# Four of twelve merge gate units made among the recurrent heads, and attention groups with 96 instead of 144 gate products

## What is computed

```python
h = rmsnorm(x, g_pre_mix)
z = h @ w_in                                   # 1024 -> 8248 columns
q_nsa, kv_nsa, g_nsa, qkv_ml, if_ml, o_ml, q_mem, g_merge = split(z)
y_nsa = gated sum of compressed, selected and window attention   # 16 heads in 4 groups
h_ml  = mlstm_chunkwise(q_m, k_m, v_m, i_pre, logf)              # 4 recurrent heads, qk after conv and silu
y_ml  = sigmoid(o_ml) * rmsnorm_per_head(h_ml)
y_mem = memory_xattn(q_mem, mem, g_mem, w_mem_kv)                # 4 heads
gm = sigmoid(g_merge.reshape(B, S, 3, 1024))
y  = gm[0] * (y_nsa @ w_proj_nsa) + gm[1] * (y_ml @ w_proj_ml) + gm[2] * (y_mem @ w_proj_mem)
x  = x + rmsnorm(y @ w_out, g_post_mix)
h  = rmsnorm(x, g_pre_ffn); x = x + (silu(gate) * up) @ w_ffn_down
```

## Time and profile before

| | |
|---|---|
| median of 3 runs | 3139.21 us (3135.36 to 3140.19) |
| the profiled execution | 3136.1 us, its span 3134.3 us |
| mean granted clock of TensorE in it | 0.962 |
| PE busy | 93% of the span |
| front | 0 to 371 us |
| attention groups | 371 to 787 us, 102 to 106 us each |
| projections and output | 787 to 942 us |
| feed-forward and second part | from there to the end |

### The profile page before, as it was taken

One profiled execution on the slowest core, in us unless ns is written; L12 is line 12 of the kernel. 1 busy time (PEld: TensorE's weight loads), 2 busy tenths in 40 slices (PEclk: granted clock), 3 DMA queues, 4 the chain that ended last, 5 costly groups with the idle time before them and its releaser, 6 DMA issues.

```text
span 3134.3 us, 34634 instructions
## 1 busy us (share of the span) xinstructions
PE 2910.9 (93%) x13386; PEld 2382.4 (76%) x13386; DVE 1513.3 (48%) x2168; ACT 887.5 (28%) x1206; POOL 341.1 (11%) x70
## 2 busy tenths in 40 slices
PE   6998799999898999899997699999999889899997
PEld 6777688888776888778885588887888765578886
DVE  2334354445457443464534845444543379555532
ACT  4333343334233222222221322122222232332211
POOL 4222111111310000000000000000000056100000
PEclk9998899899999999999998899999999999999999
DMA  6221112221441232323222122332232221122232
GB/s 193 85 67 61 54 43 83 67 71 44 144 154 54 94 106 87 101 68 106 94 93 82 51 97 94 101 101 81 94 104 91 88 68 41 55 80 94 94 98 71
DMA packets 255085, 270.43 MB, mean 86 GB/s; under 512 B 5695, under 2 KB 243407, under 8 KB 254858
## 3 DMA queue, kind: packets, MB, share of 16 engines
q1 hardware_dynamic: 250688, 261.77, 26.1%
q10 hardware_dynamic: 4298, 7.36, 0.6%
HBM read 258.62 MB, written 10.49 MB: 86 GB/s over the span
## 4 chain that ended last, share of the span: by engine, by line
PE 69%; issue 16%; DVE 6%; POOL 5%; ACT 2%; DMA 1%; SPq 0%; POOLq 0%; DVEq 0%; ACTq 0%
PE bank L1114 20%; PE bank L1115 20%; PE bank L1116 20%; POOL w_lo L1074 3%; POOL w_lo L1068 3%; PE bank L1566 1%; PE bank L1129 1%; PE bank L1131 1%; PE bank L1130 1%; DVE rstd L1989 1%; ACT w_hi L662 1%; PE bank L1142 1%; PE bank L1144 0%; PE bank L1143 0%; DVE w_lo L1954 0%
## 5 line engine op out<-in xcount | busy, mean ns | idle before, releaser
L1114 PE MATMUL bank<-h_hi,w_hi 128*128 128x512 f32 x2064 | 817.5, 396 | 53.5 <-POOL w_lo L1074 25.1
L1115 PE MATMUL bank<-h_lo,w_hi 128*128 128x512 f32 x2064 | 811.3, 393 | 0.0
L1116 PE MATMUL bank<-h_hi,w_lo 128*128 128x512 f32 x2064 | 810.6, 393 | 0.0
L1954 DVE TENSOR_TENSOR w_lo<-w_raw,w_hi 128x2048 fp32r<-128x2048 f32 (+2 forms) x176 | 390.3, 2220 | 391.7 <-ACT w_hi L662 325.7
L1114 PEld LDWEIGHTS bank<-h_hi,w_hi 128*128 128x128 f32 x2064 | 392.6, 190 | 144.5 <-POOL w_lo L1074 29.3
L1116 PEld LDWEIGHTS bank<-h_hi,w_lo 128*128 128x128 f32 x2064 | 392.5, 190 | 83.1
L1115 PEld LDWEIGHTS bank<-h_lo,w_hi 128*128 128x128 f32 x2064 | 392.9, 190 | 82.5 <-issue 1.2
L1114 PE MATMUL bank<-hid_hi,w_hi 128*128 128x512 f32 x880 | 343.5, 390 | 0.0
L1116 PE MATMUL bank<-hid_hi,w_lo 128*128 128x512 f32 x880 | 342.4, 389 | 0.0
L1115 PE MATMUL bank<-hid_lo,w_hi 128*128 128x512 f32 x880 | 342.4, 389 | 0.0
L654 ACT ACTIVATE w_hi<-w_raw 128x2048 fp32r<-128x2048 f32 x124 | 237.0, 1911 | 356.7 <-PE bank L1116 349.3
(11 more groups left out here) (355 smaller groups left out, 3489.1 us busy)
## 6 DMA issues: line engine op xcount, KB each, us to landing
w_raw<-in_ffn_w_in_dram SPq DMA_DIRECT2D x88, 1024.0 KB, 5.1
w_raw<-in_w_in_dram SPq DMA_DIRECT2D x32, 1024.0 KB, 5.4
w_raw<-in_ffn_w_out_dram SPq DMA_DIRECT2D x32, 1024.0 KB, 5.1
w_raw<-in_w_ffn_in_dram SPq DMA_DIRECT2D x22, 1024.0 KB, 5.1
w_raw<-in_ffn_w_out_dram SPq DMA_DIRECT2D x16, 768.0 KB, 4.5
w_raw<-in_conv_w_pw_dram SPq DMA_DIRECT2D x12, 1024.0 KB, 5.5
w_raw<-in_w_ffn_down_dram SPq DMA_DIRECT2D x8, 1024.0 KB, 5.1
gate_scratch<-gate_stage ACTq DMA_DIRECT2D x24, 256.0 KB, 2.0
```

The source lines that it names most:

```text
L1114: nc.tensor.matmul(bank[b][:, 0:n], wh, xh, start=first, stop=False)
L1115: nc.tensor.matmul(bank[b][:, 0:n], wh, xl, start=False, stop=False)
L1116: ins = nc.tensor.matmul(bank[b][:, 0:n], wl, xh, start=False, stop=last)
L1954: v.tensor_tensor(w_lo[slot][:, 0:n], raw[s][:, 0:n], w_hi[slot][:, 0:n].bitcast(F32), ALU.subtract).then_inc(w_lo_ready, 1)
```

## The change

Four of the twelve merge gate units, those of the third branch (memory), one for each group, become units of the front. `UNITS` has 26 entries: three of the new ones stand between, or just behind, the units qk, v and o as numbers 20, 22 and 24, and the first is 17, ahead of the last qk unit. The unit for the attention gates moves ahead of vw. In `SCHEDULE` the units 20, 22 and 24 stand between the scores and the outputs of heads 0, 1 and 2, the second output-gate unit (25) between the outputs of head 2 and the scores of head 3, and `ml_scores(2)` directly follows `ml_norm(0)`. ACT evacuates such a unit with two copies and stores both tiles with one DMA.

In the groups 96 gate products remain in four tiles. The weights of the second branch are loaded and split as two half units of 128 columns each. The first of these is split right behind the query copies, ahead of step 0, instead of at step 2. 24 gate products stand ahead of the split queries, one behind each of the 16 pairs of compressed scores, one in each step (two at the first query block of each branch), 8 and 5 in the tail. The tiles are copied out ahead of step 0, at steps 6 and 25, and at the end. The next query unit is split at step 25 instead of 32. The compressed scores go to banks 7 and 1 instead of 0 and 1, and the wait for `y_split` stands ahead of them.

```diff
          ("in", C_KV, UC, "kc"), ("in", C_KV + 256, UC, "vc"), ("in", C_KV + 512, UC, "ks"), ("in", C_KV + 1024, UC, "kw"),
-         ("in", C_KV + 768, UC, "vs"), ("in", C_KV + 1280, UC, "vw"), ("gates", 0, P, "gate"), ("gates", P, P, "if"),
-         ("in", C_QK, UC, "qk"), ("in", C_QK + 256, UC, "qk"), ("in", C_QK + 512, UC, "qk"), ("in", C_QK + 768, UC, "qk"),
-         ("in", C_V, UC, "v"), ("in", C_V + UC, UC, "v"), ("in", C_O, UC, "o"), ("in", C_O + UC, UC, "o")]
+         ("in", C_KV + 768, UC, "vs"), ("gates", 0, P, "gate"), ("in", C_KV + 1280, UC, "vw"), ("gates", P, P, "if"),
+         ("in", C_QK, UC, "qk"), ("in", C_QK + 256, UC, "qk"), ("in", C_QK + 512, UC, "qk"), ("in", C_MERGE + 2 * D, UC, "merge"),
+         ("in", C_QK + 768, UC, "qk"), ("in", C_V, UC, "v"), ("in", C_MERGE + 2 * D + UC, UC, "merge"), ("in", C_V + UC, UC, "v"),
+         ("in", C_MERGE + 2 * D + 2 * UC, UC, "merge"), ("in", C_O, UC, "o"), ("in", C_MERGE + 2 * D + 3 * UC, UC, "merge"),
+         ("in", C_O + UC, UC, "o")]
 NFIX = len(UNITS)
-FEATURE_MAJOR = ("mem_k", "q_mem", "kc", "vc", "ks", "kw", "qk")
-ACT_ONLY = ("mem_v", "gate", "if", "o")
+FEATURE_MAJOR = ("mem_k", "q_mem", "kc", "vc", "ks", "kw", "qk", "merge")
+ACT_ONLY = ("mem_v", "gate", "if", "o", "merge")
+UNIT_OF, TURN_OF = {}, []
+for _u, (_, _, _, _kind) in enumerate(UNITS):
+    TURN_OF.append(len(UNIT_OF.setdefault(_kind, [])))
+    UNIT_OF[_kind].append(_u)
 DVE_EVACS = [0]
...
-             ("ml_const", 0), ("ml_rows", 0), ("unit", 15), ("unit", 16), ("unit", 17), ("ml_cols", 0), ("unit", 18),
-             ("ml_scores", 0), ("ml_out", 0), ("unit", 19), ("ml_scores", 1), ("ml_out", 1),
-             ("unit", 20), ("ml_gain", 0), ("ml_norm", 0), ("unit", 21), ("ml_scores", 2), ("ml_out", 2), ("ml_scores", 3),
-             ("ml_gain", 1), ("ml_out", 3), ("ml_norm", 1), ("ml_turn", 0)]
+             ("ml_const", 0), ("ml_rows", 0), ("unit", 15), ("unit", 16), ("unit", 17), ("unit", 18), ("ml_cols", 0),
+             ("unit", 19), ("ml_scores", 0), ("unit", 20), ("ml_out", 0), ("unit", 21), ("ml_scores", 1), ("unit", 22), ("ml_out", 1),
+             ("unit", 23), ("ml_gain", 0), ("ml_norm", 0), ("ml_scores", 2), ("unit", 24), ("ml_out", 2),
+             ("unit", 25), ("ml_scores", 3), ("ml_gain", 1), ("ml_out", 3), ("ml_norm", 1), ("ml_turn", 0)]
...
 GATE_BANK = (4, 0)
-GATE_TILES = 6
-GATE_PRE, GATE_STEP = 18, 3
-GATE_EVAC = {8: 0, 16: 1, 24: 2, 32: 3}
+GATE_TILES, ALL_TILES = 4, 6
+GATE_PRE, GATE_CMP, GATE_TAIL = 24, 1, (8, 5)
+GATE_STEP = [2 if qb == 0 else 1 for br, qb, hh in STEPS] + [1] * 3
+GATE_EVAC = {6: 1, 25: 2}
+HALF = KT * P
...
             with sp.Fori(0, GROUPS) as g:
-                def gate_load(b):
-                    load(g * 2 + (U_NSA // 2 + (b + 1) // 2), (b + 1) % 2, w_in_t[:, :, bass.ds(g * UC + (C_MERGE + b * D), UC)], KT, UC)
+                def half_gate_load(t):
+                    load(g * 2 + (U_NSA // 2 + 1), t, w_in_t[:, :, bass.ds(g * UC + (C_MERGE + D + t * P), P)], KT, P)
                 load(g * 2 + U_NSA // 2, 0, w_in_t[:, :, bass.ds(g * UC, UC)], KT, UC)
-                gate_load(0)
-                gate_load(1)
+                load(g * 2 + U_NSA // 2, 1, w_in_t[:, :, bass.ds(g * UC + C_MERGE, UC)], KT, UC)
+                half_gate_load(0)
+                sp.wait_ge(gt_front_stored, 16 * GROUPS)
                 sp.wait_ge(y_split, g * 2 + 2)
                 for b in range(2):
                     for i in range(2):
                         for half in range(2):
                             sp.dma_start(k_st[b][i][DH * half:DH * (half + 1), :].bitcast(F32),
                                          k_scratch[b, i, bass.ds(g * DH, DH), :]).then_inc(kd_landed, 16)
-                gate_load(2)
+                half_gate_load(1)
...
+                    act.wait_ge(evac_act, u + 1)
+                    g = TURN_OF[u]
+                    act.dma_start(g_scratch[g * ALL_TILES + 4:g * ALL_TILES + 6, :, :].rearrange("t p n -> p t n"), gt_front[:, :, :]
+                                  ).then_inc(gt_front_stored, 16)
                 if kind == "qk":
...
                     nc.scalar.activation(q_st[half, h, :], bank[0][half, :], ACT.Copy).then_inc(q_high, 1)
+                high_in_loop(g * 2 + (U_NSA // 2 + 1), 0, 0, HALF)
...
                 def gate_evac(m):
-                    if m % 2 == 0:
-                        act.wait_ge(gt_half, g * 3 + (m // 2 + 1))
+                    if m == 0:
+                        act.wait_ge(gt_half, g + 1)
                     else:
-                        act.wait_ge(w_used, g * 4 + (U_NSA + m // 2 + 2))
-                    act.wait_ge(gt_stored[m % 2], g * 48 + 16 * (m // 2 + 1))
+                        act.wait_ge(w_used, g * 4 + (U_NSA + m + 1))
+                    act.wait_ge(gt_stored[m % 2], g * 32 + 16 * (m // 2 + 1))
                     nc.scalar.activation(gt_stage[m % 2][:, :], bank[GATE_BANK[m % 2]][:, :], ACT.Copy).then_inc(gt_copied, 1)
                     act.wait_ge(gt_copied, g * GATE_TILES + (m + 3))
-                    act.dma_start(g_scratch[bass.ds(g * GATE_TILES + m, 1), :, :].rearrange("a p n -> p (a n)"),
+                    act.dma_start(g_scratch[bass.ds(g * ALL_TILES + m, 1), :, :].rearrange("a p n -> p (a n)"),
                                   gt_stage[m % 2][:, :]).then_inc(gt_stored[m % 2], 16)
+                gate_evac(0)
                 for i in range(NS + 2):
                     if i < NS:
...
-                    if i == 2:
-                        high_in_loop(g * 2 + (U_NSA // 2 + 1), 0, 0)
                     if i in GATE_EVAC:
                         gate_evac(GATE_EVAC[i])
                         if GATE_EVAC[i] == 1:
-                            high_in_loop(g * 2 + (U_NSA // 2 + 1), 1, 1)
-                        if GATE_EVAC[i] == 3:
+                            high_in_loop(g * 2 + (U_NSA // 2 + 1), 1, 1, HALF)
+                        if GATE_EVAC[i] == 2:
                             high_in_loop(g * 2 + (U_NSA // 2 + 2), 0, 0)
                 act.wait_ge(c_t, g + 1)
                 for qb in range(TT):
                     ins = nc.scalar.activation(pT_c[:, HPG * qb:HPG * (qb + 1), :],
...
+                gate_evac(3)
...
                 for n in range(4):
-                    low_in_loop(g * 4 + (U_NSA + 1 + n), (n + 1) % 2)
...
-                    b, t = m // 2, m % 2
-                    s, out_ = (b + 1) % 2, bank[GATE_BANK[t]][:, :]
+                    s, out_ = (1, 1, 0, 1)[m], bank[GATE_BANK[m % 2]][:, :]
+                    cols, c0 = (UC, m * P) if m < 2 else (P, 0)
                     if first == 0:
                         pe.wait_ge(gt_copied, g * GATE_TILES + (m + 1))
-                        if t == 0:
-                            pe.wait_ge(w_lo_ready, g * 4 + (U_NSA + 2 + b))
+                        if m != 1:
+                            pe.wait_ge(w_lo_ready, g * 4 + (U_NSA + max(m, 1) + 1))
                     for n in range(first, last):
                         k, part = n // 3, n % 3
-                        c = k * UC + t * P
+                        c = k * cols + c0
                         ins = nc.tensor.matmul(out_, (w_lo if part == 2 else w_hi)[s][:, c:c + P],
                                                (h_lo if part == 1 else h_hi)[:, k, :], start=n == 0, stop=n == 3 * KT - 1)
                     if last == 3 * KT:
-                        ins.then_inc(gt_half if t == 0 else w_used, 1)
+                        ins.then_inc(gt_half if m == 0 else w_used, 1)
...
                 pe.wait_ge(q_split, g + 1)
+                pe.wait_ge(y_split, g * 2 + 2)
...
                         c = NCP * (2 * qb + hh // 2)
-                        ins = stacked(bank[hh % 2][:, c:c + NCP], hh, qb, [kc_st[0][:, :], kc_st[1][:, :]])
-                ins.then_inc(c_s, 1)
+                        ins = stacked(bank[OUT_BANK[hh % 2]][:, c:c + NCP], hh, qb, [kc_st[0][:, :], kc_st[1][:, :]])
+                        if hh == HPG - 1 and qb == TT - 1:
+                            ins.then_inc(c_s, 1)
+                        gates(GATE_CMP)
                 pe.wait_ge(kd_landed, g * 128 + 128)
-                pe.wait_ge(y_split, g * 2 + 2)
...
-                    gates(GATE_STEP)
+                    gates(GATE_STEP[i])
...
                 ins.then_inc(c_t, 1)
-                gates(12)
```

More of the change, by code:

```diff
@@ L1412, in _ @@
                 ins.then_inc(c_t, 1)
-                gates(12)
+                gates(GATE_TAIL[0])
                 pe.wait_ge(c_ta, g + 1)
@@ L1420, in _ @@
                 ins.then_inc(c_o, 1)
[L1421 removed]
+                gates(GATE_TAIL[1])
                 pe.wait_ge(y_done, g + 1)
@@ L1685, in unit @@
                     dve.wait_ge(evac_act, u + 1)
-                    for j in range(2 * (u - 14), 2 * (u - 14) + 2):
+                    for j in range(2 * TURN_OF[u], 2 * TURN_OF[u] + 2):
                         acc = conv_acc[j % 2][:, :]
```

58 lines of the change are left out of this document (32 added, 26 removed).

## The result

The changed kernel takes 3149.1 us (median of 8 runs, 3146.1 to 3153.6), the kernel before 3135.6 us beside it. The ratio is 1.0038, with a 95% interval of 1.0027 to 1.0049, so it is 12 us **slower**, where 3129 us and "faster" were forecast. The profiled execution took 3149.0 us, its span is 3147.2 us, 12.9 us longer than before.

What follows compares the result with a forecast made beforehand. PE's own stream bounds the attention groups; chains that PE waits for bound the recurrent stage. First group 31.6 us later, four groups -41.6, sum -10.0 on the 3139.2 us median: 3129 us, range 3112 to 3142.

Steps and rivals of the forecast that it cites:

- A group, new waits: Attention group: waits of 2.1, 1.2 and 0.9 us in the steps, low clock 1.0, and 0.8 at the next query unit.
- Front: Before the groups: four moved units add 44.4 us, partly filling waits; first group starts 31.6 us later (25 to 38).
- new wait of head 2: Front, scores of head 2: DVE's norm delays the decay arguments and PE, +4.3 us, and low clock +1.7.
- head 3's 2.5 us: Front, head 3: following a unit as head 2 did, its start to outputs and its outputs shorten, -2.5 us.
- Group, what leaves: Each group: 62 gate products leave the steps -14.3 us, split moved from under cmp_mask -2.7, cold stretches -3.5.
- hold of step 25: Group steps: gate copy and full split hold ACT 3.1 us, PE waits 2.1 us; low clock behind it 1.0.
- step 6: Group steps: gate copy with a half split holds ACT about 2.1 us in steps of 1.1 us, +1.2 us.
- first steps: Start of a group's steps: DVE's masks and compressed softmax need 1.2 us a step against PE's 1.0, +0.9 us.
- It comes out even: Rival: the group steps become chains, another 2 us a group, 3137 us; chance 0.18.
- Slower: Rival: with fewer large gate products in the steps, 10 us more per group at 1.2 GHz, 3148 us; chance 0.13.
- The rule on transposes: Rival: transposes do not count as busy PE, so all group steps run at 1.2 GHz, 3325 us; chance 0.02.
- The criteria: Signs of failure: group starts 96 us or more apart, or first group after 410 us; expected granted clock 0.95 or above.

Runs made afterwards that it cites:

- e5: e4 with the gain and norm of heads 0 and 1 moved behind unit 24, after the scores of head 2: 3101.2 us, ratio 0.9894.
- e4: Changed kernel with the edits of e1, e2 and e3 together: 3108.5 us, ratio 0.9915 to the kernel before.
- e9: Kernel before with ACT's copy of turned probabilities ahead of exp, and step 2's full split done ahead of the steps: 3111.7 us, ratio 0.9917.
- e1: Changed kernel with ACT's copy of the turned probabilities of step i-2 ahead of the exp of step i: 3135.0 us, ratio 0.9996.
- e2: Changed kernel with the third gate copy and the full weight split moved from step 25 to step 32: 3136.0 us, ratio 1.0005.
- e3: Changed kernel with the second gate copy and the half weight split moved from step 6 to step 12: 3139.1 us, ratio 1.0009.
- e10: Changed kernel with only the full split moved to step 32: 3137.1 us, ratio 0.9995; its window columns are length, PE busy, PEclk, DMA, GB/s.

## Why the prediction was wrong

The step that failed is "A group, new waits". It put 5.2 us a group to waits and low clock in the steps, where the runs show 10.9. It left out the order of ACT's two operations in steps that nothing holds, and the hold of GpSimd's split on DVE's gain product, and took half of what the clock cost behind step 25.

**Front: right, and 5 us better than forecast.** 26.4 us for 31.6, inside the bounds of 25 to 38. The waits of the earlier trace rows and of the start of head 3 are gone. The memory heads gave 6.8 us for 5.2. Heads 0 and 1 gave 3.7 each where 2.7 net was forecast, as the merge units there ran at full clock throughout (11.0 us each) and the outputs behind them took 2.39 us. The new wait of head 2 was there (from the broadcast to the merge unit 4.0 us more than at head 1, for 4.3), and e5 shows that its cause was the one named:

```profile
345.98 2.11 PE L1308 MATMUL bank<-qk_in 128*128 128x256 f32 x4 [4.94 <-DVE s_ml L1794]
347.74 0.77 PE L1134 MATMUL bank<-h_hi,w_hi 128*128 128x512 f32 x1
...
381.14 4.14 PE L1319 MATMUL bank<-v_ml,s_ml 128*128 128x129 f32 x20 [1.21 <-DVE s_ml L1794]
393.95 1.97 PE L1329 MATMUL bank<-identity_ones,h_ml 128*128 128x128 f32 x8 [7.80 <-DVE h_ml L1819]
```

Of head 3's 2.5 us only 0.9 came: its outputs still ran at the low clock, 4.14 us. The same instructions behind the same waits took 2.50 us at head 2 of the kernel before, so this term was a guess on the clock.

**Group, what leaves: right.** The terms -14.3, -2.7 and -3.5 say that the steps lose 20.5 us; from the kernel before to e4 they lost 19.2. Between e9 and e4, which differ in the steps mainly by the same 62 products, it is 13.7 us, 2.2 of them by the low clock that e9 still has at the start of its steps, behind the 32 small products, and e4 has not. The gate products between the compressed scores cost 3.5 us for 4.4; queries and tail together +0.9 for +0.5.

**Group, new waits: here it failed.** The prediction put 5.2 us there (hold of step 25 with its clock 3.1, step 6 1.2, first steps 0.9). e4 against the changed kernel shows 10.9 in the steps. By ranges of steps, means of the four groups in us:

| steps | 0 to 9 | 10 to 13 | 14 to 26 | 27 to 30 | 31 to 34 | all |
|---|---|---|---|---|---|---|
| changed kernel | 13.2 | 8.9 | 20.7 | 11.7 | 6.7 | 61.2 |
| e1 | 11.6 | 10.0 | 19.4 | 11.3 | 6.3 | 58.5 |
| e2 | 13.2 | 9.8 | 20.7 | 7.8 | 6.7 | 58.2 |
| e3 | 12.8 | 7.4 | 20.8 | 10.4 | 6.7 | 58.2 |
| e4 | 11.1 | 6.7 | 19.3 | 6.8 | 6.3 | 50.3 |

- *Hold of step 25*: 2.1 forecast for the wait and 1.0 for the clock; 3.9 in e2 behind step 25. The mechanism was right and the wait of 2.66 us nearly so. The clock cost 2.1, twice the 1.0, inside the bounds of 0 and 2.8.
- *Step 6*: 1.2 forecast, 1.9 in e3 up to step 13, and more where the clock falls behind the wait (e2 and e1 have 9.8 and 10.0 us at steps 10 to 13). I counted the hold of ACT and not the split that it starts on POOL. I had read from the earlier trace rows that a split blocks DVE's products of two SBUF operands, and took that only as something that goes. I did not ask which such product the moved, smaller split would meet. That is the gain of the first output block, two steps on.
- *ACT's order in steps that nothing holds*: nothing forecast. In e1 it is worth 3.8 us outside steps 10 to 13, of which the longer wait for DVE there takes back 1.1. I followed ACT's strict order only where it is held, at steps 6 and 25, and summed step lengths elsewhere. But the order "exp, then copy" in itself sets the least time between scores(i) and the weighing of i-2. Steps 3 and 5 of the changed kernel took 1.9 and 1.7 us, those of e1 1.0 each.
- *First steps*: 0.9 forecast, for DVE's load. In the changed kernel no such wait shows, but when ACT's order is put right a wait of 0.89 us for DVE's copy stands at step 6 (e1 and e4). The term was there, beneath a larger one. It and one of 0.6 us at step 22 are still in e4, and are the 1.3 us by which the removals seem to fall short.

With these 1.3 us, that is 7.0 us in the steps of each group, less 0.4 elsewhere in it, so 26.5 us for the four. 5.2 us came back in front, the merge stage took 4.8, and the rest gave 3.2: -10.0 + 26.5 - 5.2 + 4.8 - 3.2 = 12.9 us more than before. The last two are no part of the mechanism, for the code there is the same: what follows the merge took 2217.8 us in this profile and 2219.5 to 2221.1 us in the twelve others.

**The rivals.** "It comes out even" named the mechanism, steps that become chains, and priced it at 2 us a group where e1's median shows 3.3. "Slower" named the time, 3148 us, for a reason that the trace denies: worked out from the granted clocks of the windows (twice what is missing to 1, times the length), PE was at 1.2 GHz for 44 us in the first, third and fourth group, and for 46 us in those of the earlier trace rows. That the time came near 3148 us is no point for it. The rule on transposes in the Trainium skill, "TensorE: Matmul & The Clock Gate", section "Part 4: PE-mode transpose", did not act as that rival feared: most steps of e4 hold one gate product among transposes and small products, and its window over the steps of the third group (columns as in e10's) shows the full clock:

```profile
605.00:650.00 45.00, 43.25 (x314) 1.00 0.09 29
```

**The criteria** did their work: starts 100 us apart are beyond the 96 that the prediction gave as its failure. The granted clock of the groups, 0.92 to 0.93, is below the 0.95 that it expected as well; the low clock came behind the waits and at the ends of the groups.

## What to carry to other kernels

Filler products between pipelined steps do two things: they fill, and they give every chain of a step its time. Before taking them out, work out the least step length that each engine's own order of instructions allows (here scores, mask, exp, copy), not only its load. And when an instruction is moved, follow what it starts: a weight split of ACT set off 2.4 us of GpSimd, which held a product of four columns on VectorE for all of its length; moving it away from there was worth 9 us. Last, give the kernel before the same care, before an advantage is put down to the new layout, and look at what it already does right: the tail of nine products was in it.
